# Depthwise convolution taps on TensorE: from 128-wide diagonals built on the chip to four 64x64 tiles with diagonals loaded from DRAM

## The chip, the cores and the metric

One Trainium2 chip, one core of it. The metric is the device time of one execution in microseconds; lower is better. TensorE multiplies, VectorE (DVE), ScalarE (ACT) and GpSimd (POOL) work element by element, SyncE (SP) issues DMAs. The engines run their instruction queues in order and meet by semaphores.

## What is computed

Two stacks of two layers each, on 256 tokens of width 1024, in float32. The first stack has attention, an RWKV recurrence and gated spatial mixing; the second has a feed-forward, a mixer and a second feed-forward in each layer. The change is in the mixer of the second stack, of which this is the part that matters:

```python
q, k, v, c, g = jnp.split(u @ w_in[i], splits, axis=-1)
q = rms_norm_2(q.reshape(B, S, N_HEADS, HEAD_DIM), q_norm[i])
k = rms_norm_2(k.reshape(B, S, KV_HEADS, HEAD_DIM), k_norm[i])
y_attn = window_attention(q, k, v, sink[i], rel_bias) @ w_attn_out[i]
c_val, c_gate = jnp.split(c, 2, axis=-1)
c = c_val * jax.nn.sigmoid(c_gate)
c = depthwise_conv(c, conv_w[i], conv_b[i])     # 31 taps, 512 channels, along the tokens
c = jax.nn.silu(layer_norm_2(c, conv_ln_g[i], conv_ln_b[i]))
y_conv = c @ w_conv_out[i]
g_attn, g_conv = jnp.split(jax.nn.sigmoid(g), 2, axis=-1)
h = h + (g_attn * y_attn + g_conv * y_conv) @ w_o[i]
```

## The kernel before

Activations lie features first: 128 features on the partitions, 256 tokens along a row. The weights come from DRAM in tiles of 128x128, eight to a block (512 KB). A block goes through four engines: SP loads it (`raw`, seven buffers), ScalarE rounds it (`hi`, five buffers), VectorE takes the remainder (`lo`, in place of `raw`), and TensorE does three matmuls for each tile (`lo` by the high part of the activations, `hi` by the high part, `hi` by the low part). ScalarE casts block b + 5 when TensorE has ended block b, since a buffer is free only then; VectorE splits block b + 4 at that point of its queue.

`main_order` lists the work in one order for all engines; each engine's program walks through it. Beside the main line there are side chains (`Flow.chain`): lists of steps with `"next"` between them. At the end of every block `tick` runs each chain on to its next `"next"`, on every engine at its own place in its queue. Attention (`att2_steps`) and the convolution (`conv2_steps`) of the mixer are such chains: what one engine does in step n is used by another in step n or n + 1, and nothing but the queues' order and semaphores ties them.

The convolution's input `Cb` holds four chunks of 128 channels, 286 tokens wide with the padding. Of the 31 taps VectorE does 20 (`CV`), as multiply and add of a shifted row into `cacc`. TensorE does the other 11, each as one float32 matmul of a 128x128 diagonal by 256 columns of `Cb`, accumulated in bank 4 (`CONV`). ScalarE builds the 88 diagonals (identity by a weight), three in each step, in eight buffers. After each pair of chunks VectorE adds the bank to `cacc` (`conv sum`). Then come mean, square, variance, norm, SiLU and the split in high and low part (`ych`, `ycl`), one step each; `conv out` multiplies these by its weights and waits for `("split", l, k // 2)`.

In a mixer the main line is: `c` 0 to 3 (projection of the convolution's input, chain `conv2` started behind `c` 2), `rcol`, `qkv` 0 to 2, `v2`, `qk norm` (matmuls for the norm of queries and keys, then ScalarE and VectorE), attention's chain started, eight `gate2` of two blocks each, `attn out` (four blocks), `conv out` (four blocks), `wo`. Attention's steps, twice: scores, maximum (VectorE), exponential (ScalarE), reciprocal (VectorE), scaling (ScalarE), transposes (`turn`, TensorE), product with the values. Banks of PSUM are taken in turn from pools: `MAIN` is 0, 1, 3 and `ATT2` is 5, 6, 7, 2.

The levels of the RWKV recurrence in the first stack already use tiles of 64x64, in the order and with the banks of this loop (`left` and `right` pick 64 rows of two operands):

```python
for n in range(4):
    for g, s in ((0, 0), (0, 1), (1, 0), (1, 1)):
        rows, into = (slice(64 * t, 64 * t + 64) for t in (s, s ^ g))
        h = 2 * n + g
        i = pe.mm(outs[g][into, n * w:(n + 1) * w], left(h, rows), right(h, rows), True, True)
```

L198 is the helper that issues every matmul, L202 transposes, L250 ScalarE's operations, L205 and L213 VectorE's `tensor_tensor` and `scalar_tensor_tensor`. Most tensors besides the weights lie in one big tile, `arena`, and the profile calls them all by that name.

Of the kernel before, what the change touches and what calls it, by code (L numbers as in the profile page):

```python
# [9 lines left out]
ACT = mybir.ActivationFunctionType  # L10
# [10 lines left out]
L = 2  # L21
# [4 lines left out]
CW, CV = 31, 20  # L26
NT1 = 58 * 8 + 24 * 4 + 64 + 44 * 8 + 22 * 8
# [20 lines left out]
PARG = [("norm_final", 8)]  # L48

# [366 lines left out]
def build(nc, T):  # L416
# [3 lines left out]
    with ctx:  # L420
# [27 lines left out]
        def un(a, n):  # L448
            return ar[:, a * 256:(a + n) * 256]
# [43 lines left out]
        def signal(name, step=1):  # L493
# [10 lines left out]
        d_x = [signal(f"dma_x{i}", 16) for i in range(2)]  # L504
        d_hank = [signal(f"dma_hank{i}", 16) for i in range(8)]
        d_af = [signal(f"dma_first_ada{i}", 16) for i in range(FIRST)]
        d_ada = [signal(f"dma_ada{i}", 16) for i in range(RAWA)]
        d_crow, d_par0, d_par, d_cst0, d_cst1, d_cst, d_lora, d_small, d_b2, d_scr, d_p, d_pp, d_pq, d_out = (
            signal(f"dma_{n}", 16) for n in ("c_row", "par0", "par", "cst0", "cst1", "cst", "lora", "small", "bias2", "scr", "p", "p_out",
                                             "p_back", "out"))  # L510
# [94 lines left out]
        diag = [un(61, 4)[:, i * 128:(i + 1) * 128] for i in range(8)]  # L605
# [14 lines left out]
        def tensor_program(e):  # L620
# [419 lines left out]
            def conv2(l):  # L1040
                taps = [0]

                def step(what, *q):
                    if what == "pe tap":
                        pr, m, j = q
                        if (m, j) == (pr, CV):
                            take(CONV, ("conv", l, pr))
                        d = diag[taps[0] % 8]
                        taps[0] += 1
                        pe.wait_ge(a_cv, ("diag", l, m, j))  # L1050
                        pe.wait_ge(v_main, ("c", l, m))
                        pe.mm(t256(ps(("conv", l, pr)), m - pr), d, Cb[:, m, j:j + 256], j == CV, j == CW - 1).then_inc(
                            pe_cv, ("tap", l, m, j))
                    elif what == "mean":
# [44 lines left out]
            for item in ORDER:  # L1099
# [192 lines left out]
        def vector_program(e):  # L1292
# [365 lines left out]
            def conv2(l):  # L1658
                def w(m, j):
                    return P("conv_w_2", l, j * 4 + m)  # L1660

                def step(what, *q):
                    if what == "taps":
                        pr, j0 = q
                        for j in range(j0, min(j0 + 2, CV)):
                            for m in (pr, pr + 1):
                                o = t256(cacc, m)
                                if j == 0:
                                    v.wait_ge(v_main, ("c", l, m))
                                    x = v.ts(o, Cb[:, m, 0:256], w(m, 0), P("conv_b_2", l, m), MUL, ADD)  # L1670
                                else:
                                    v.wait_ge(v_cv, ("tap", l, m, j - 1))
                                    x = v.stt(o, Cb[:, m, j:j + 256], w(m, j), o, MUL, ADD)
                                x.then_inc(v_cv, ("tap", l, m, j))
                    elif what == "conv sum":
                        pr = q[0]
                        o = cacc[:, pr * 256:(pr + 2) * 256]
                        v.wait_ge(pe_cv, ("tap", l, pr + 1, CW - 1))
                        v.wait_ge(v_cv, ("tap", l, pr + 1, CV - 1))
                        v.tt(o, o, ps(("conv", l, pr)), ADD).then_inc(v_cv, ("conv sum", l, pr), frees=("conv", l, pr))  # L1680
                        if pr == 2:
                            v.wait_ge(v_cv, ("conv sum", l, 2))
                            v.tt(cy2[:, 0:512], cacc[:, 0:512], cacc[:, 512:1024], ADD).then_inc(v_cv, ("conv half", l))
                            v.wait_ge(v_cv, ("conv half", l))
                            v.tt(cy2[:, 0:256], cy2[:, 0:256], cy2[:, 256:512], ADD).then_inc(v_cv, ("conv total", l))
# [51 lines left out]
            for item in ORDER:  # L1737
# [251 lines left out]
                elif what == "gate2":  # L1989
# [3 lines left out]
                    v.wait_ge(pe_main, item)  # L1993
                    v.tt(two(dst), two(ps(item)), bc(var_t, 1, [128, 2, 256]), MUL).then_inc(v_main, item, frees=item)
# [41 lines left out]
        def scalar_program(e):  # L2036
# [262 lines left out]
            def conv2(l):  # L2299
                built = [0]  # L2300

                def step(what, *q):
                    if what == "diag":
                        pr, m, j = q
                        n = built[0]
                        built[0] += 1
                        if n >= 8:
                            a.wait_ge(pe_cv, ("tap", l, *conv_taps[n - 8]))
                        a.wait_ge(d_cst1, "cst1")
                        a.act(diag[n % 8], C("ident"), ACT.Identity, scale=P("conv_w_2", l, j * 4 + m)).then_inc(  # L2310
                            a_cv, ("diag", l, m, j))
                    elif what == "square":
# [20 lines left out]

            conv_taps = [(m, j) for pr in (0, 2) for m in (pr, pr + 1) for j in range(CV, CW)]
# [31 lines left out]
            for item in ORDER:  # L2366
# [201 lines left out]
                elif what == "conv2":  # L2568
                    f.chain(item, conv2_steps(q[0]), conv2(q[0]))
                elif what == "rcol":  # L2570
                    a.wait_ge(pe_main, item)
                    a.act(rcol, adab[:, 0:2], ACT.Copy).then_inc(a_main, item, frees=item)
                elif what == "qkv":
                    l, p = q
                    f.tiles(16 if p < 2 else 8)
                    if p == 2:
# [20 lines left out]
                elif what == "attention2":  # L2597
                    f.chain(("att2", q[0]), att2_steps(q[0]), attention2(q[0]), True)
# [120 lines left out]
        def sync_program(e):  # L2719
# [51 lines left out]
            for item in ORDER:  # L2771
# [82 lines left out]
                elif what == "f first":  # L2854
                    pass
                elif what == "ple":
# [73 lines left out]

def modulation(inputs):
# [12 lines left out]
def program(nc):  # L2944
    def din(name, shape):
# [6 lines left out]
             vmask=din("vmask", (8, 512)), flip=din("flip", (128, 128)), p=din("p", (L, 128, 512)))  # L2952
# [31 lines left out]
```

## Time and profile before

| | |
|---|---|
| median of 3 runs | 2149.69 us (2148.77 to 2149.78) |
| profiled execution | 2149.16 us, span 2147.4 us |
| TensorE busy | 2120.1 us (99%) |
| VectorE busy | 1680.6 us (78%) |
| ScalarE busy | 1265.4 us (59%) |
| GpSimd busy | 13.1 us (1%) |
| granted TensorE clock | 1.00 |
| DMA | 415.12 MB, mean 193 GB/s |

Busy shares are means over stages of different kinds. The span runs from the first to the last instruction; the execution's own time is 1.8 us longer. A float32 matmul has two records in the trace. Rows of the timeline that belong together are merged, with their count; matmuls overlap, so that a merged row ends some 0.28 us after its last start.

### The profile page before, as it was taken

How to read it: one execution, taken by the hardware profiler on the slowest of the kernel's cores; microseconds unless marked ns; L12 is line 12 of the kernel's file. 1: busy time of each engine (PE TensorE's matmuls, PEld its weight loads, DVE VectorE, ACT ScalarE, POOL GpSimd, SP SyncE). 2: the span in 40 equal slices, each digit the busy share in tenths (PEclk: the TensorE clock that was granted, in tenths of full speed). 3: DMA queues.
4: the chain of work that ended last, by engine and by line, in shares of the span. 5: the costliest groups of instructions: out<-in, count | busy, mean ns of one | idle time of the engine just before them, and what ended most of it. 6: DMA issues, size and time to landing. Idle time of an engine off the chain costs nothing.

```text
span 2147.4 us, 38873 instructions
## 1 busy us (share of the span) xinstructions
PE 2120.1 (99%) x16094; PEld 1934.2 (90%) x16094; DVE 1680.6 (78%) x2642; ACT 1265.4 (59%) x2122; POOL 13.1 (1%) x20
## 2 busy tenths in 40 slices
PE   8999999999999999999999999999999999999999
PEld 7898989999998899998888999888898889998888
DVE  7888698887877698776886677887688767878875
ACT  4765556555855755555655567665466545766554
POOL 0000000000000000000000000000000000000000
PEclk9999999999999999999999999999999999999999
DMA  9555577777644477555555533555555553346554
GB/s 371 192 194 174 173 244 258 240 244 276 215 158 168 158 253 231 186 186 186 180 193 187 168 117 132 203 191 191 187 177 191 192 186 128 124 164 205 191 191 129
DMA packets 116371, 415.12 MB, mean 193 GB/s; under 512 B 13105, under 2 KB 16561, under 8 KB 115682
## 3 DMA queue, kind: packets, MB, share of 16 engines
q1 hardware_dynamic: 116194, 412.63, 57.0%
q8 instruction: 127, 2.08, 0.4%
q14 instruction: 50, 0.41, 0.1%
HBM read 409.42 MB, written 3.16 MB: 192 GB/s over the span
## 4 chain that ended last, share of the span: by engine, by line
PE 91%; ACT 4%; DVE 3%; DMA 1%; issue 1%; SPq 0%; ACTq 0%; DVEq 0%
PE bank L198 90%; ACT arena L250 2%; DMA raw<-W 1%; DVE arena L205 1%; DVE lo L205 1%; ACT hi L250 1%; PE bank L202 1%; DVE ada L222 0%; ACT L250 0%; DVE arena L213 0%; ACT L242 0%; DMA xT<-x 0%; DVE h L205 0%; DVE ysl L205 0%; SPq L195 0%
## 5 line engine op out<-in xcount | busy, mean ns | idle before, releaser
L198 PE MATMUL bank<-h,hi 128*128 128x256 f32 (+1 forms) x5344 | 1223.0, 314 | 0.0
L250 ACT ACTIVATE hi<-raw 128x1024 fp32r<-128x1024 f32 x656 | 689.2, 1056 | 563.0 <-PE bank L198 500.7
L198 PE MATMUL bank<-h,lo 128*128 128x256 f32 x3440 | 986.1, 287 | 3.5 <-DVE h L205 3.5
L198 PEld LDWEIGHTS bank<-h,hi 128*128 128x128 f32 x5344 | 880.1, 190 | 67.1 <-issue 2.6
L205 DVE TENSOR_TENSOR lo<-raw,hi 128x1024 fp32r<-128x1024 f32 x656 | 793.1, 1220 | 90.7 <-ACT hi L250 89.8
L198 PEld LDWEIGHTS bank<-h,lo 128*128 128x128 f32 x3440 | 654.6, 190 | 15.1 <-issue 7.0
L198 PE MATMUL bank<-act,hi 128*128 128x512 f32 x1056 | 370.0, 393 | 0.0
L198 PE MATMUL bank<-act,lo 128*128 128x256 f32 x1056 | 294.7, 279 | 0.0
L198 PEld LDWEIGHTS bank<-act,hi 128*128 128x128 f32 x1056 | 197.9, 187 | 47.1
L198 PEld LDWEIGHTS bank<-act,lo 128*128 128x128 f32 x1056 | 197.9, 187 | 0.0
L250 ACT ACTIVATE arena<-arena 128x256 f32<-128x256 f32 (+4 forms) x202 | 98.5, 493 | 158.6 <-DVE arena L205 151.2
L250 ACT ACTIVATE arena<-bank 128x256 f32<-128x256 f32 (+3 forms) x428 | 173.6, 449 | 11.7 <-PE bank L198 10.1
L198 PE MATMUL bank<-arena 64*64 64x64 f32 (+7 forms) x2674 | 165.7, 272 | 7.0 <-ACT arena L250 3.9
L198 PEld LDWEIGHTS bank<-arena 64*64 64x64 f32 (+3 forms) x2674 | 123.6, 145 | 30.1 <-issue 8.5
L205 DVE TENSOR_TENSOR arena<-arena 128x256 f32<-128x256 f32 (+2 forms) x222 | 117.8, 535 | 20.7 <-ACT arena L250 16.9
L213 DVE SCALAR_TENSOR_TENSOR arena<-arena,par 128x256 f32<-128x256 f32 x260 | 116.0, 486 | 19.4 <-ACT arena L250 16.2
L205 DVE TENSOR_TENSOR act<-arena,act 128x256 fp32r<-128x256 f32 x132 | 56.0, 424 | 84.3 <-ACT act L250 83.9
L222 DVE CUSTOM_DVE_ANT_0 ada<-ada,crow,par 128x1024 f32<-128x1024 f32 x80 | 103.5, 1293 | 0.6 <-DMA ada<-WA 0.4
L205 DVE TENSOR_TENSOR arena<-bank,arena 128x256 f32<-128x256 f32 (+2 forms) x181 | 68.7, 423 | 3.6 <-ACT arena L250 3.6
L213 DVE SCALAR_TENSOR_TENSOR xT<-bank,xT 128x256 f32<-128x256 f32 x96 | 40.6, 422 | 35.1 <-PE bank L198 33.5
L250 ACT ACTIVATE act<-arena 128x256 fp32r<-128x256 f32 x132 | 52.9, 401 | 4.8 <-DVE arena L205 4.8
L198 PE MATMUL bank<-ysh,lo 128*128 128x256 f32 x192 | 55.6, 289 | 0.0
(150 smaller groups left out, 1891.6 us busy)
## 6 DMA issues: line engine op xcount, KB each, us to landing
raw<-W SPq DMA_DIRECT2D x664, 512.0 KB, 3.3
ada<-WA SPq DMA_DIRECT2D x80, 512.0 KB, 3.6
arena<-WA SPq DMA_DIRECT2D x16, 512.0 KB, 14.1
p_projected<-arena SPq DMA_DIRECT2D x2, 1024.0 KB, 7.3
arena<-scr SPq DMA_DIRECT2D x16, 128.0 KB, 4.7
arena<-p_projected SPq DMA_DIRECT2D x2, 1024.0 KB, 4.8
xT<-x SPq DMA_DIRECT2D x2, 512.0 KB, 4.9
arena<-lora SPq DMA_DIRECT2D x2, 512.0 KB, 10.3
```

Of the source, the lines that this page charges most:

```text
L198: return self.done(lambda e: e.matmul(out, l, r, start=start, stop=stop, skip_group_check=True))
L202: return self.done(lambda e: e.transpose(out, in_, ident[0:n, 0:n]))
L205: return self.done(lambda e: e.tensor_tensor(out, a, b, op))
L213: return self.done(lambda e: e.scalar_tensor_tensor(out=out, in0=a, scalar=s, in1=b, op0=o0, op1=o1))
L222: return self.done(lambda e: e.tensor_tensor_reduce(out, a, b, 1.0, start, MUL, ADD, total))
L250: return self.done(lambda e: e.activation(out, in_, f, scale=scale, **kw))
```

## The change

Each tap's diagonal is cut in two halves of 64 channels. A tap is now two matmuls of 64x64 by 256 columns. For every second tap the two tiles are those on the array's diagonal, (rows 0-63, outputs 0-63) and (64-127, 64-127), and read `Cb`. For the others they are the two off it, (0-63, 64-127) and (64-127, 0-63), and read a copy of `Cb` in which channels 0-63 and 64-127 of each chunk are exchanged. The two kinds add up in two banks. The copies are made by eight DMAs in all, on ScalarE's queue, when a pair of chunks is there. The diagonals are an input now (`taps`, 1.4 MB a layer) and are loaded by SP at `mixer2`. The 44 matmuls of a pair of chunks stand in one piece: behind `rcol`, and behind `qkv` 0. VectorE adds two banks for each pair, in two steps. `qkv` goes 2, 0, 1 instead of 0, 1, 2, and on ScalarE attention's steps stand ahead of the convolution's.

```diff
 def conv2_steps(l):
-    s = []
-    for pair in (0, 2):
-        todo = [(m, j) for m in (pair, pair + 1) for j in range(CV, CW)]
-        built = []
-        for j in range(0, CV, 2):
-            s += [("taps", pair, j)]
-            if j >= 4:
-                s += [("pe tap", pair, *t) for t in built.pop(0)]
-            built.append(todo[:3])
-            del todo[:3]
-            s += [("diag", pair, *t) for t in built[-1]] + ["next"]
-        assert not any(built), built
-        s += [("conv sum", pair)]
-    return s + ["next", ("mean",), "next", ("square",), "next", ("var",), "next", ("norm",), ("silu",), "next", ("split",)]
+    s = [("taps", 0, 0, 4), "next", ("taps", 0, 4, 8), "next", ("conv sum", 0, 0), "next", ("taps", 0, 8, 12), "next"]
+    s += [("taps", 2, 0, 4), "next", ("conv sum", 2, 0), "next"]
+    for pair, n in ((0, 12), (2, 4)):
+        while n < 2 * CV:
+            s += [("taps", pair, n, min(n + 4, 2 * CV)), "next"]
+            n += 4
+    return s + [("conv total",), "next", ("mean",), "next", ("square",), "next", ("var",), "next", ("norm",), ("silu",), "next", ("split",)]
...
-        s += [("mixer2", l), ("c", l, 0), ("c", l, 1), ("c", l, 2), ("conv2", l), ("c", l, 3), ("c last", l), ("rcol", l)]
-        s += [("qkv", l, p) for p in range(3)] + [("v2", l), ("qk norm", l), ("attention2", l)]
+        s += [("mixer2", l), ("c", l, 0), ("c", l, 1), ("c", l, 2), ("turned", l, 0), ("conv2", l), ("c", l, 3), ("c last", l)]
+        s += [("turned", l, 2), ("rcol", l), ("taps", l, 0), ("qkv", l, 2), ("qkv", l, 0), ("taps", l, 2), ("qkv", l, 1)]
+        s += [("v2", l), ("qk norm", l), ("attention2", l)]
...
+                elif what == "taps":
+                    l, pr = q
+                    outs = [take(ATT2, ("conv", l, pr, d)) for d in range(CG)]
+                    pe.wait_ge(d_taps, ("taps", l))
+                    pe.wait_ge(d_turn[pr // 2], ("turned", l, pr))
+                    pe.wait_ge(v_main, ("c", l, pr + 1))
+                    for m in (pr, pr + 1):
+                        for n in range(CT):
+                            d = tap_turn(m, n)
+                            for r in range(CG):
+                                c = (r + d) % CG
+                                rows, into = slice(CS * r, CS * r + CS), slice(CS * c, CS * c + CS)
+                                i = pe.mm(t256(outs[d], m - pr)[into, :], tapw[rows, m, n, :], Ct[d][rows, m, CV + n:CV + n + 256],
+                                          (m - pr) * CT + n < CG, False)
+                    i.then_inc(pe_main, ("conv", l, pr))
...
+                        pr, first = q
                         o = cacc[:, pr * 256:(pr + 2) * 256]
...
+                        v.wait_ge(pe_main, ("conv", l, pr))
+                        for d in range(first, first + 2):
+                            use = ("conv", l, pr, d)
+                            v.wait_ge(v_cv, before[pr])
+                            v.tt(o, o, ps(use), ADD).then_inc(v_cv, use, frees=use)
+                            before[pr] = last_use[pr] = use
...
+                elif what == "turned":
+                    l, pr = q
+                    a.wait_ge(v_main, ("c", l, pr + 1))
+                    for d in range(1, CG):
+                        n = CS * d
+                        for out, src in ((slice(0, 128 - n), slice(n, 128)), (slice(128 - n, 128), slice(0, n))):
+                            a.dma(Ct[d][out, pr:pr + 2, :], Cb[src, pr:pr + 2, :]).then_inc(d_turn[pr // 2], item)
...
-                    f.chain(("att2", q[0]), att2_steps(q[0]), attention2(q[0]), True)
+                    f.chain(("att2", q[0]), att2_steps(q[0]), attention2(q[0]))
...
+                elif what == "mixer2":
+                    l = q[0]
+                    s.wait_ge(pe_main, ("f down 1", l, 7))
+                    s.dma(tapw.rearrange("p m n i -> p (m n i)"), T["taps"][l]).then_inc(d_taps, ("taps", l))
```

TensorE, layer 0, behind `rcol` (the 128x1 matmuls); before, a block of `qkv` 0 runs to the first three taps, in bank 4:

```order
L198 MATMUL bank2<-cst_72,rs_t_76 128x1 x2
L198 MATMUL bank1<-h_71,lo2_63 128x256
L198 MATMUL bank1<-h_71,hi1_57 128x256 x2
...
L198 MATMUL bank4<-arena_80 128x256 x3
L198 MATMUL bank1<-h_71,lo3_64 128x256
L198 MATMUL bank1<-h_71,hi2_58 128x256 x2
```

and now (22 rows of two matmuls each, banks 5 and 6 in turn, then the weights of `qkv` 2):

```order
L204 MATMUL bank2<-cst_72,rs_t_76 128x1 x2
L204 MATMUL bank5<-arena_80 64x256 x2
L204 MATMUL bank6<-arena_80 64x256 x2
...
L204 MATMUL bank1<-h_71,lo2_63 128x256
L204 MATMUL bank1<-h_71,hi1_57 128x256 x2
```

All 44 matmuls of a pair of chunks now stand ahead of a block of weights, and no taps are left between the later blocks.

ScalarE, layer 0, at attention's first exponential (`arena_80,sml_75<-`, eight times) and the scaling behind it; before, with three diagonals (`<-cst_72,par_73`) in each step:

```order
L250 ACTIVATE hi1_57<-raw3_52 128x1024
L250 ACTIVATE arena_80<-cst_72,par_73 128x128 x3
L250 ACTIVATE sml_75<-sml_75 128x8
L250 ACTIVATE arena_80,sml_75<-arena_80,sml_75 128x256 x8
L250 ACTIVATE hi2_58<-raw4_53 128x1024
L250 ACTIVATE arena_80<-cst_72,par_73 128x128 x3
L250 ACTIVATE arena_80<-arena_80,sml_75 128x256 x8
```

and now:

```order
L256 ACTIVATE hi1_57<-raw3_52 128x1024
L256 ACTIVATE sml_75<-sml_75 128x8
L256 ACTIVATE arena_80,sml_75<-arena_80,sml_75 128x256 x8
L256 ACTIVATE hi2_58<-raw4_53 128x1024
L256 ACTIVATE arena_80<-arena_80,sml_75 128x256 x8
```

The diagonals are gone, and the order of the rest is the same.

VectorE, layer 0, at the end of the convolution's chain; the rows with `bank` are the evictions of `attn out` 0 to 3, one a block, `arena_80<-arena_80 128x1024` is the convolution's norm. Before:

```order
L205 TENSOR_TENSOR arena_80<-arena_80 128x1024
L213 SCALAR_TENSOR_TENSOR arena_80<-arena_80,bank3 128x512
L205 TENSOR_TENSOR lo1_62<-raw1_50,hi3_59 128x1024
L205 TENSOR_TENSOR ycl_86<-arena_80,ych_85 128x512 x2
L213 SCALAR_TENSOR_TENSOR arena_80<-arena_80,bank0 128x512
L205 TENSOR_TENSOR lo2_63<-raw2_51,hi4_60 128x1024
```

and now:

```order
L211 TENSOR_TENSOR lo2_63<-raw2_51,hi4_60 128x1024
L211 TENSOR_TENSOR arena_80<-arena_80 128x1024
L219 SCALAR_TENSOR_TENSOR arena_80<-arena_80,bank1 128x512
L211 TENSOR_TENSOR lo3_64<-raw3_52,hi0_56 128x1024
L211 TENSOR_TENSOR ycl_86<-arena_80,ych_85 128x512 x2
L219 SCALAR_TENSOR_TENSOR arena_80<-arena_80,bank3 128x512
```

Norm and split stand two blocks later; the split is now ahead of the eviction of the last `attn out`.

## Rows read from the trace of the kernel before

**Rows 1.** The page's part 1: busy us, share of the span, instructions.
```profile
PE 2120.1 (99%) x16094; PEld 1934.2 (90%) x16094; DVE 1680.6 (78%) x2642; ACT 1265.4 (59%) x2122; POOL 13.1 (1%) x20
```

**Rows 2.** Busy time by stretches of layer 0's mixer; the first row names the columns.
```profile
core 0: us, PE busy (x) PEld busy (x) DVE busy (x) ACT busy (x) POOL busy (x), PEclk, DMA share, GB/s
1221.48:1249.61 28.13, 28.13 (x210) 27.15 (x210) 21.19 (x40) 15.83 (x31) 0.00 (x0) 1.00 0.35 115
1249.61:1262.18 12.57, 12.57 (x88) 11.21 (x86) 8.27 (x14) 5.90 (x9) 0.00 (x0) 1.00 0.36 123
1262.18:1282.44 20.26, 20.26 (x156) 19.32 (x155) 19.55 (x37) 17.01 (x44) 0.00 (x0) 1.00 0.41 131
1282.44:1311.22 28.78, 28.78 (x221) 26.53 (x219) 24.51 (x44) 20.77 (x51) 0.00 (x0) 1.00 0.33 110
1311.22:1334.40 23.18, 22.18 (x182) 20.95 (x181) 15.10 (x19) 19.78 (x27) 0.00 (x0) 1.00 0.41 136
```

**Rows 3.** Timeline: three taps between blocks (PE), and casts at blocks' ends (ACT).
```profile
1229.15 1.46 PE L198 MATMUL bank<-arena 128*128 128x256 f32 x6
1233.32 1.46 PE L198 MATMUL bank<-arena 128*128 128x256 f32 x6
...
1337.54 1.06 ACT L250 ACTIVATE hi<-raw 128x1024 fp32r<-128x1024 f32 x1 [1.82 <-PE bank L198]
1340.42 1.06 ACT L250 ACTIVATE hi<-raw 128x1024 fp32r<-128x1024 f32 x1 [1.82 <-PE bank L198]
```

**Rows 4.** Timeline of TensorE around one RWKV level, and its matmuls by form.
```profile
132.31 0.40 PE L198 MATMUL bank<-h,hi 128*128 128x256 f32 x2
132.64 1.57 PE L198 MATMUL bank<-arena 64*64 64x64 f32 x64
...
134.36 0.40 PE L198 MATMUL bank<-h,hi 128*128 128x256 f32 x2
...
L198 PE MATMUL bank<-arena 64*64 64x128 f32 x32 | 1.1, 269 | 0.0
L198 PE MATMUL bank<-arena 64*64 64x64 f32 x32 | 0.7, 224 | 0.0
```

**Rows 5.** Timeline: VectorE's and ScalarE's part of attention, first half.
```profile
1253.91 1.68 DVE L213 SCALAR_TENSOR_TENSOR arena<-arena,par 128x1024 f32<-128x1024 f32 x2 [8.10 <-ACT arena L250]
1256.64 1.67 DVE L213 SCALAR_TENSOR_TENSOR arena<-arena,par 128x256 f32<-128x256 f32 x4
1258.23 1.22 DVE L205 TENSOR_TENSOR lo<-raw,hi 128x1024 fp32r<-128x1024 f32 x1
1263.34 2.48 DVE L213 SCALAR_TENSOR_TENSOR arena<-bank,arena 128x512 f32<-128x512 f32 x4 [0.58 <-PE bank L198]
1268.91 2.28 DVE L225 TENSOR_REDUCE sml<-arena 128x8 f32<-128x2048 f32 x1
1277.95 0.21 DVE L219 RECIPROCAL sml<-sml 128x8 f32<-128x8 f32 x1
...
1278.81 3.29 ACT L250 ACTIVATE arena<-arena,sml 128x256 f32<-128x256 f32 x8
```

**Rows 6.** Timeline of ScalarE: the second half's scaling.
```profile
1307.09 3.29 ACT L250 ACTIVATE arena<-arena,sml 128x256 f32<-128x256 f32 x8
```

**Rows 7.** Timeline: cast ahead of SiLU (ACT), and both splits behind it (DVE).
```profile
1326.39 1.04 ACT L250 ACTIVATE hi<-raw 128x1024 fp32r<-128x1024 f32 x1
...
1330.53 0.69 DVE L205 TENSOR_TENSOR ycl<-arena,ych 128x512 fp32r<-128x512 f32 x1 [1.84 <-ACT ych L250]
1332.18 0.69 DVE L205 TENSOR_TENSOR ycl<-arena,ych 128x512 fp32r<-128x512 f32 x1 [0.96 <-ACT ych L250]
```

**Rows 8.** Timeline of TensorE: the convolution's variance, layer 0.
```profile
1322.38 0.67 PE L198 MATMUL bank<-arena,cst 128*128 128x256 f32 x2 [0.99 <-DVE arena L205]
```

**Rows 9.** DMA issues (KB each, median us to landing); gating of the second chunk.
```profile
raw<-W SPq DMA_DIRECT2D x664, 512.0 KB, 3.3
arena<-scr SPq DMA_DIRECT2D x16, 128.0 KB, 4.7
arena<-lora SPq DMA_DIRECT2D x2, 512.0 KB, 10.3
...
1217.29 0.43 DVE L213 SCALAR_TENSOR_TENSOR arena<-arena 128x256 f32<-128x256 f32 x1 [0.76 <-ACT arena L250]
```

More of the change, by code:

```diff
@@ L26 @@
 CW, CV = 31, 20
+CG = 2
+CT, CS = CW - CV, 128 // CG
 NT1 = 58 * 8 + 24 * 4 + 64 + 44 * 8 + 22 * 8
@@ L48, with tap_turn @@
 PARG = [("norm_final", 8)]
+def tap_turn(m, n):
+    return (m % 2 * CT + n) % CG
 def par_columns():
@@ L504, in build @@
         d_x = [signal(f"dma_x{i}", 16) for i in range(2)]
+        d_turn = [signal(f"dma_turned{i}", 16) for i in range(2)]
         d_hank = [signal(f"dma_hank{i}", 16) for i in range(8)]
@@ L507, in build @@
         d_ada = [signal(f"dma_ada{i}", 16) for i in range(RAWA)]
-        d_crow, d_par0, d_par, d_cst0, d_cst1, d_cst, d_lora, d_small, d_b2, d_scr, d_p, d_pp, d_pq, d_out = (
+        d_crow, d_par0, d_par, d_cst0, d_cst1, d_cst, d_lora, d_small, d_b2, d_scr, d_p, d_pp, d_pq, d_taps, d_out = (
             signal(f"dma_{n}", 16) for n in ("c_row", "par0", "par", "cst0", "cst1", "cst", "lora", "small", "bias2", "scr", "p", "p_out",
-                                             "p_back", "out"))
+                                             "p_back", "taps", "out"))
         negw0, halfa0 = sml[:, 32:40], sml[:, 40:48]
@@ L604, in build @@
         cacc, cyc, cy2 = un(16, 4), un(20, 4), un(24, 4)
-        diag = [un(61, 4)[:, i * 128:(i + 1) * 128] for i in range(8)]
+        Ct = [Cb] + [ar[:, 73 * 256 + i * 1144:73 * 256 + (i + 1) * 1144].rearrange("p (m t) -> p m t", m=4) for i in range(CG - 1)]
+        tapw = un(78, 11)[:, 0:4 * CT * CS].rearrange("p (m n i) -> p m n i", m=4, n=CT)
         pf, pfh, pfl = un(49, 2), alias("pfh", 51, 2), alias("pfl", 57, 2)
@@ L1040, in conv2 @@
             def conv2(l):
-                taps = [0]
                 def step(what, *q):
[L1044 to L1054, printed above, removed]
+                    if what == "mean":
                         o = take(CONV, ("cmean", l))
@@ L1658, in conv2 @@
             def conv2(l):
+                before, last_use = {}, {}
                 def w(m, j):
@@ L1663, in step @@
                     if what == "taps":
[L1664 to L1674, printed above, removed]
+                        pr, first, last = q
@@ new lines, in step @@
+                        for n in range(first, last):
+                            j, m = n // 2, pr + n % 2
+                            o = t256(cacc, m)
+                            if j == 0:
+                                v.wait_ge(v_main, ("c", l, m))
+                                x = v.ts(o, Cb[:, m, 0:256], w(m, 0), P("conv_b_2", l, m), MUL, ADD)
+                            else:
+                                v.wait_ge(v_cv, last_use.pop(pr) if pr in last_use else ("tap", l, m, j - 1))
+                                x = v.stt(o, Cb[:, m, j:j + 256], w(m, j), o, MUL, ADD)
+                            x.then_inc(v_cv, ("tap", l, m, j))
+                            before[pr] = ("tap", l, m, j)
@@ L1675, in step @@
                     elif what == "conv sum":
-                        pr = q[0]
+                        pr, first = q
                         o = cacc[:, pr * 256:(pr + 2) * 256]
[L1678 to L1685, printed above, removed]
+                        v.wait_ge(pe_main, ("conv", l, pr))
@@ new lines, in step @@
+                        for d in range(first, first + 2):
[3 more added lines that the diff above has]
+                            before[pr] = last_use[pr] = use
+                    elif what == "conv total":
+                        v.wait_ge(v_cv, ("tap", l, 3, CV - 1))
+                        v.tt(cy2[:, 0:512], cacc[:, 0:512], cacc[:, 512:1024], ADD).then_inc(v_cv, ("conv half", l))
+                        v.wait_ge(v_cv, ("conv half", l))
+                        v.tt(cy2[:, 0:256], cy2[:, 0:256], cy2[:, 256:512], ADD).then_inc(v_cv, ("conv total", l))
@@ L1993, in vector_program @@
                     v.wait_ge(pe_main, item)
+                    v.wait_ge(pe_main, ("conv", l, 2))
                     v.tt(two(dst), two(ps(item)), bc(var_t, 1, [128, 2, 256]), MUL).then_inc(v_main, item, frees=item)
@@ L2299, in conv2 @@
             def conv2(l):
-                built = [0]
                 def step(what, *q):
[L2303 to L2312, printed above, removed]
+                    if what == "square":
                         a.wait_ge(v_cv, ("cmean", l))
@@ L2332, in conv2 @@
                 return step
-            conv_taps = [(m, j) for pr in (0, 2) for m in (pr, pr + 1) for j in range(CV, CW)]
             def merge(name, l, m, h):
@@ L2928, in stream, with tap_weights @@
     return out.reshape(nblk, 128, BT * 128)
+def tap_weights(inputs):
+    w = np.asarray(inputs["conv_w_2"], np.float32).reshape(L, CW, 4, CG, CS)
+    out = np.zeros((L, CG, CS, 4, CT, CS), np.float32)
+    i = np.arange(CS)
+    for m in range(4):
+        for n in range(CT):
+            for r in range(CG):
+                out[:, r, i, m, n, i] = w[:, CV + n, m, (r + tap_turn(m, n)) % CG, :]
+    return out.reshape(L, 128, 4 * CT * CS)
 def modulation(inputs):
@@ L2951, in program @@
              oneh=din("oneh", (32, 512)), relb=din("relb", (32, 8)),
-             vmask=din("vmask", (8, 512)), flip=din("flip", (128, 128)), p=din("p", (L, 128, 512)))
+             vmask=din("vmask", (8, 512)), flip=din("flip", (128, 128)), p=din("p", (L, 128, 512)), taps=din("taps", (L, 128, 4 * CT * CS)))
     T["out"] = nc.dram_tensor("out", [128, 2048], F32, kind="ExternalOutput").ap()
@@ L2978 @@
         crow=np.ascontiguousarray(crow), lnb=np.ascontiguousarray(np.repeat(ln[:, None, :], 128, axis=1)), bs=bs,
-        oneh=oneh, relb=np.ascontiguousarray(inputs["rel_bias_2"]), vmask=vmask, flip=flip,
+        taps=tap_weights(inputs), oneh=oneh, relb=np.ascontiguousarray(inputs["rel_bias_2"]), vmask=vmask, flip=flip,
         p=np.stack([features_first(inputs["p_2"][l, 0]) for l in range(L)]))
```

2 lines of the change are left out of this document (1 added, 1 removed).

## The prediction

> **What bounds the kernel now.** I read the page first: TensorE is busy for 2120.1 of 2147.4 us, VectorE for 78% [rows 1]. The reader is to see that a microsecond taken from TensorE's queue is a microsecond of the end, as long as the others keep up. So the table by stretches comes next, for the mixer of layer 0 of the second block, where the convolution's taps run [rows 2]. TensorE is never idle there but for 1.0 us in the last stretch. VectorE, though, is busy for 19.55 of the 20.26 us between the first scores and the first transposes of attention: it follows TensorE with almost nothing to spare. Layer 1 repeats layer 0 565.5 us later, so everything is counted twice.
>
> I call eight weight tiles a block, as the kernel does. Without taps a block takes TensorE 2.88 us (the `hi` casts of ScalarE, each waiting for the end of a block, start 2.88 us apart); with three taps between two blocks the period is 4.17 us [rows 3]. So a tap costs (4.17 - 2.88) / 3 = 0.43 us, 0.435 with the switches.
>
> **What is removed from TensorE.** 11 taps x 4 chunks x 2 layers = 88 matmuls x 0.435 = 38.3 us, 18 of each layer's 44 before the q/k norm, 26 behind it.
>
> **What is added.** 176 matmuls of 64x64 by 256 columns, in four blocks of 44. The trace has this very pattern: the levels of the RWKV inverse (`quarters`) issue 64x64 tiles in the same order, two into one bank and two, with halves exchanged, into another, in float32 too. One such burst has 16 matmuls of 64 columns and 16 of 128 (32 records each) [rows 4]. At 0.427 us for 256 columns (a tap without its share of the switches) a column is 1.67 ns; one after another, 16 x 64 + 16 x 128 columns would be 5.1 us. The burst costs 134.36 - 132.31 less three steps of 0.12 us, which the weight matmuls between take anyway, 1.7 us. With four at once it is 1.28 us plus 0.4 us of switch and tail; with two at once 2.56 us already. So four run at once, and a new block is 44 x 0.427 / 4 + 0.4 = 5.1 us, four of them 20.4 us. TensorE alone thus gains 38.3 - 20.4 = 17.9 us.
>
> On a rule that speaks against this: of the burst the rows show 1.7 us, with both row halves writing one bank. The Trainium skill (TensorEngine Tiling (Array Packing), Restrictions and Gotchas) says that different row tiles can't access one PSUM bank at the same time. By that rule two would run at once, a block would be 9.8 us, and the sum 18.8 us higher; this trace does not agree with it.
>
> Also gone: 88 diagonals on ScalarE. Added on VectorE: four sums of bank and accumulator instead of two in each layer, near 0.6 us each. Neither is on TensorE's path by itself. The load of the diagonals (1.4 MB on SP's queue) stands behind a wait that ends with the same matmul as the block before it, so SP loses nothing; it is used 20 us later, and the weights, at 3.3 us to landing [rows 9], are asked for seven blocks ahead. I cost both at nothing.
>
> **Where cover is lost.** The steps of attention and convolution run once a block on every engine. Taps stretched a block to 4.17 us for TensorE; now it is 2.88. VectorE does in such a block a `lo` split (1.13 us), four taps (1.59) and half an eviction (0.3), 3.0 us, and more where attention has its steps. I count from T, the start of the q/k norm's matmuls (1249.61 before).
>
> First transposes: VectorE's chain starts at T + 4.3, when ScalarE has the norm [rows 5]. From there VectorE has no gap: norm 1.6, two blocks of split and taps and an eviction 6.0, a split 1.13, so it is at the scores at T + 13.1, while TensorE, without the 1.8 us of taps, starts them at T + 10.8. Evictions of scores 2.4, taps 1.6, split 1.1, maximum 2.8: T + 21.0 (22.2 before). From there to the reciprocal are taps, eviction, split, taps, split: 6.4 us, as in the rows; ScalarE's eight scalings add 3.3. The probabilities are ready at T + 30.9. TensorE is there, five blocks after scores, at T + 27.2. Before, the scalings ended at 1282.10 and the transposes began at 1282.44 [rows 2, 5]: 0.3 us to spare. New wait: 3.7 us.
>
> Second transposes: counted on in the same way, scores at T + 35.5, maximum T + 44.9, ScalarE's exponentials from T + 46.3 (behind the `hi` cast that waits for TensorE) to 50.4, reciprocal 51.9, scalings 55.3; TensorE is there at T + 53.8. Before, 0.8 us were to spare (1310.39 against 1311.22) [rows 2, 6]. New wait: 1.5 us.
>
> End of the convolution: the new steps put SiLU at step 27 and the split at step 28, where they were 25 and 26, and step 28 is the last block of `attn out`. ScalarE comes to SiLU only when TensorE has ended block 27, and then does cast, table load, SiLU, copy. From the start of that cast to the end of the first `ycl` are 4.8 us, to the second 6.5 (1326.39 to 1332.87) [rows 7]. TensorE has 2.88 us of block 28 left and 0.72 us of `conv out` before it wants the second half: 6.5 - 3.6 = 2.9 us of wait, where there was none.
>
> The variance of the convolution waited 1.0 us before [rows 8]; `ysh` and a table load no longer stand in its way, and I count 0.4 us.
>
> **Sum.** Each layer: taps -19.15, blocks +10.2, waits 3.7 + 1.5 + 2.9 + 0.4 - 1.0 = +7.5: -1.4 us. Two layers: -2.8 us. The profiled execution took 2149.16 us with a span of 2147.4; against the median of the runs, 2149.69, I forecast 2147.0 us. TensorE's saving is thus mostly handed to waits. For each of the new waits the bounds are nothing and twice its size: 0 to 16 us a layer; I take the worked values, since 0.3 and 0.8 us of slack before are measured.
>
> **The first copy with halves exchanged** can start at 1217.7, when VectorE has the second chunk gated; TensorE wants it behind `rcol`, at 1222.1 [rows 2, 9]. There are 4.4 us. Nearest rows: 3.3 us for the weights, 4.7 for 128 KB from DRAM, 10.3 for `lora`. By the first two it costs 0 to 0.3 us a layer, by the last 5.9. It is 143 KB, near the second; I take nothing.
>
> **The rivals.**
> - A, the waits as worked out: 2147.0, itself between 2142 and 2152. 0.60.
> - B, VectorE and ScalarE keep up better, so that one or more waits stay away: with none, 2149.7 - 17.9 = 2131.8; with only that of `conv out`, 2137.6. For it: 0.7 us of VectorE's stretch was idle. Against: the slack before was 0.3 us where TensorE now comes 3.9 us (nine taps) sooner. 0.20.
> - C, slower: the copies land late. At 10.3 us, 2147.0 + 11.8 = 2158.8; it decides once they need over 8 us. For it: 128 pieces of 1.1 KB beside the weights' stream; against: 128 KB in 4.7. 0.15.
> - D, the tiles do not overlap as in the RWKV burst, two at once: 2147.0 + 18.8 = 2165.8. The change would then save TensorE nothing at all. Against: [rows 4]. 0.05.
>
> **Numbers.** 0.2% is 4.3 us, about what a measurement of this kernel can tell from no change. Below 2145.4: 0.18 of A, 0.17 of B, 0.35. Above 2154.0: 0.02 of A, 0.12 of C, all of D, 0.19. Between, 0.46. The range of 8 in 10 takes in A and the edges of B and C: 2138 to 2156.
>
> **What would show it.** Four bursts of 5.1 us with 44 matmuls each; TensorE idle 3 to 4 us ahead of the first transposes behind scalings of ScalarE, 1 to 2 us ahead of the second, about 3 us in two pieces at `conv out` behind VectorE's `ycl`; VectorE without a gap from T + 4.3 to the maximum. TensorE's busy time down by about 18 us and its idle time up by 15. I am wrong if the first transposes wait for nothing, if a burst takes over 7 us, if TensorE waits for the copy, or if after a wait of 3.7 us the granted clock, 1.00 in all stretches here [rows 2], is found at 1.2 GHz for a while, which no row of before prices.

## The result and the profile after

| | before | after |
|---|---|---|
| median | 2148.81 us (20 runs, 2148.16 to 2149.78) | 2152.58 us (20 runs, 2150.70 to 2156.82) |
| profiled execution, span | 2147.4 us | 2149.9 us |
| granted TensorE clock | 1.00 | 0.997 |

The ratio is 1.0019, with an interval of 1.0012 to 1.0025: 3.8 us slower, where 2.7 us faster was forecast (2147.0 against the 2149.69 known then). The page of the changed kernel has these rows (part 1; the first line of the chain that ended last; two of the DMA issues):

```profile
PE 2110.8 (98%) x16270; PEld 1921.0 (89%) x16270; DVE 1683.1 (78%) x2646; ACT 1238.0 (58%) x2032; POOL 13.1 (1%) x20
...
PE 87%; ACT 6%; DVE 5%; DMA 1%; issue 1%; SPq 0%; ACTq 0%; DVEq 0%
...
arena<-taps SPq DMA_DIRECT2D x2, 1408.0 KB, 8.3
...
arena<-arena ACTq DMA_DIRECT2D x8, 143.0 KB, 2.6
```

TensorE's busy time fell from 2120.1 us [rows 1] by 9.3 us only, where about 18 were to go. Busy time counts slow matmuls as well as many, so this is the first sign that something other than waiting took time back. The copies land in 2.6 us.

TensorE's timeline in layer 0, its waits and the landmarks that answer to [rows 2, 4, 7, 8]. The number in brackets is the idle time ahead of the row and what ended it:

```profile
1221.26 4.98 PE L204 MATMUL bank<-arena 64*64 64x256 f32 x88
...
1251.08 2.36 PE L204 MATMUL bank<-arena,cst 128*128 128x512 f32 x6
...
1282.37 3.26 PE L208 MATMUL bank<-cst,arena 128*128 128x128 f32 x16 [3.80 <-ACT arena L256]
...
1308.33 1.94 PE L208 MATMUL bank<-cst,arena 128*128 128x128 f32 x16 [0.95 <-ACT arena L256]
...
1324.82 0.67 PE L204 MATMUL bank<-arena,cst 128*128 128x256 f32 x2 [0.56 <-DVE arena L211]
...
1333.45 0.36 PE L204 MATMUL bank<-ych,lo 128*128 128x256 f32 x1 [2.22 <-DVE ycl L211]
1335.01 0.58 PE L204 MATMUL bank<-ych,lo 128*128 128x256 f32 x1 [0.39 <-DVE ycl L211]
```

The burst has no wait ahead of it and takes 4.98 us. T, the start of the q/k norm, is 1251.08, and this execution was 0.75 us ahead of the other up to `rcol`, so T came 2.2 us later by the change. All the new waits are there, 3.8, 0.95, 0.56 and 2.2 + 0.4 us. One thing in these rows is not a wait: the same sixteen transposes take 3.26 us behind the long wait and 1.94 behind the short one.

Windows of 1 us of the same kernel say why; the column to read is PEclk, the granted clock, the third number from a row's end (0.50 is 1.2 GHz, 1.00 is 2.4 GHz):

```profile
core 0: us, PE busy (x) PEld busy (x) DVE busy (x) ACT busy (x) POOL busy (x), PEclk, DMA share, GB/s
1281.00:1282.00 1.00, 0.00 (x0) 0.00 (x0) 1.00 (x2) 1.00 (x4) 0.00 (x0) 1.00 0.24 94
1282.00:1283.00 1.00, 0.63 (x5) 0.66 (x6) 1.00 (x4) 1.00 (x3) 0.00 (x0) 0.90 0.00 0
1283.00:1284.00 1.00, 1.00 (x7) 1.00 (x6) 1.00 (x3) 1.00 (x2) 0.00 (x0) 0.50 0.06 16
...
1285.00:1286.00 1.00, 1.00 (x6) 1.00 (x6) 1.00 (x3) 1.00 (x4) 0.00 (x0) 0.50 0.00 0
1286.00:1287.00 1.00, 1.00 (x10) 1.00 (x9) 1.00 (x3) 1.00 (x3) 0.00 (x0) 0.90 0.00 0
1287.00:1288.00 1.00, 1.00 (x11) 1.00 (x10) 1.00 (x2) 0.09 (x1) 0.00 (x0) 1.00 0.00 0
...
1334.00:1335.00 1.00, 0.62 (x4) 0.33 (x2) 0.73 (x2) 1.00 (x2) 0.00 (x0) 0.50 0.01 4
...
1336.00:1337.00 1.00, 1.00 (x7) 1.00 (x6) 0.69 (x1) 0.00 (x0) 0.00 (x0) 0.50 0.07 16
```

The clock is at half for 3.4 us from 1282.8 on, behind the wait of 3.80 us, and again for 3.4 us in the second stretch, behind 2.22 us; it stays at 1.00 behind 0.95 us. At half the clock a window holds 6 or 7 records of matmuls instead of 10 or 11, so such a stretch costs about half of what TensorE works in it, 1.7 us in the first and, with 0.39 us of the second wait inside it, 1.5 in the other. Layer 1 has the same two stretches. The Trainium skill (TensorE: Matmul & The Clock Gate, Why this matters for your kernels) tells to avoid long idle gaps between bursts of matmuls, since the clock goes back to half behind them. The trace agrees for 3.80 us, and here the clock also fell behind 2.22 us.

What held the first transposes is seen in the chain that ended last, followed through this place (start, us, what; VectorE from the scores' eviction, whose row also holds four taps, to the reciprocal, then the scalings on ScalarE):

```profile
1264.63 3.98 DVE arena L219 x8
1268.60 1.14 DVE lo L211
1269.74 2.21 DVE sml L231
...
1272.54 1.58 DVE arena L219 x4
1274.12 0.60 DVE arena L211
1274.73 1.13 DVE lo L211
1275.86 1.58 DVE arena L219 x4
1277.44 1.14 DVE lo L211
...
1278.69 0.21 DVE sml L225
...
1279.34 2.90 ACT arena L256 x7
```

VectorE has no gap there. Between maximum and reciprocal stand eight taps (two rows of 1.58 us), an eviction of `gate2` (0.60) and two splits of weights. The taps are the convolution's work, in front of attention's.

### The profile page after: what moved, and what is told of

Its sections match the earlier page's. It is cut to its first block, busy times and chain, and to the rows that moved or that the text cites. A ratio compares the mean times of both kernels' runs of the same rounds, so it can differ in the third digit from the quotient of the medians.

```text
span 2149.9 us, 39148 instructions
## 1 busy us (share of the span) xinstructions
PE 2110.8 (98%) x16270; PEld 1921.0 (89%) x16270; DVE 1683.1 (78%) x2646; ACT 1238.0 (58%) x2032; POOL 13.1 (1%) x20
## 4 chain that ended last, share of the span: by engine, by line
PE 87%; ACT 6%; DVE 5%; DMA 1%; issue 1%; SPq 0%; ACTq 0%; DVEq 0%
PE bank L204 86%; ACT arena L256 4%; DVE lo L211 1%; DVE arena L219 1%; ACT hi L256 1%; DVE arena L211 1%; PE bank L208 1%; DMA raw<-W 1%; ACT L256 0%; DVE ada L228 0%; DMA xT<-x 0%; DVE sml L231 0%; ACT L248 0%; ACT ych L256 0%; DVE h L211 0%
## 5 line engine op out<-in xcount | busy, mean ns | idle before, releaser
L204 PE MATMUL bank<-arena 64*64 64x64 f32 (+7 forms) x2850 | 142.1, 278 | 6.9 <-ACT arena L256 3.9
L204 PEld LDWEIGHTS bank<-arena 64*64 64x64 f32 (+2 forms) x2850 | 105.5, 141 | 31.0 <-issue 8.8
L219 DVE SCALAR_TENSOR_TENSOR arena<-arena,par 128x256 f32<-128x256 f32 x260 | 115.9, 485 | 14.0 <-ACT arena L256 10.8
## 6 DMA issues: line engine op xcount, KB each, us to landing
arena<-WA SPq DMA_DIRECT2D x16, 512.0 KB, 13.8
```

The costliest lines, as they stand in the source:

```text
L204: return self.done(lambda e: e.matmul(out, l, r, start=start, stop=stop, skip_group_check=True))
L219: return self.done(lambda e: e.scalar_tensor_tensor(out=out, in0=a, scalar=s, in1=b, op0=o0, op1=o1))
```

## The experiments

The theory: the change took from TensorE what it should; the time went into two waits in each layer, and each of them costs more than its length, since the clock is at half behind it. Rivals: that the 64x64 bursts are themselves dearer than they look or slow what runs beside them; that the tiles do not run four at once; that the waits come of the bursts or the added sums and not of where the steps stand.

| run | median us | ratio to before (interval) |
|---|---|---|
| e1_warm | 2147.76 | 0.9997 (0.9988 to 1.0005) |
| e2_ahead | 2144.54 | 0.9983 (0.9974 to 0.9992) |
| e3_merged | 2142.99 | 0.9975 (0.9966 to 0.9985) |
| e4_both | 2135.00 | 0.9938 (0.9926 to 0.9950) |
| e5_straight | 2172.11 | 1.0106 (1.0092 to 1.0120) |
| e6_late | 2157.70 | 1.0039 (1.0025 to 1.0053) |
| e7_22 | 2131.38 | 0.9918 (0.9905 to 0.9932) |

### e1_warm: TensorE busy in the waits

The changed kernel with added matmuls on constants, whose result nobody reads, in front of the two long waits.

```diff
+            def warm(use, n):
+                o = take(CONV, use)
+                pe.wait_ge(d_cst, "cst")
+                for i in range(n):
+                    pe.mm(o[:, 0:256], C("ones"), C("cos"), True, True)
...
                     elif what == "turn":
+                        if p == 0:
+                            warm(("warm", l, 0), 8)
...
                     l, p = q
+                    if p == 0:
+                        warm(("warm", l, 1), 6)
```

Expected:

> The changed kernel, plus matmuls whose result nobody reads, into the idle bank 4: eight float32 ones of 256 columns (3.5 us) ahead of the first transposes of attention and six (2.6 us) ahead of conv out. They fill TensorE's two long waits and shorten neither. Theory (the missing 3.1 us of each layer are the granted clock, down to half for some 3.4 us behind each of the two long waits): the clock stays at 1.00, the transposes take 1.9 us instead of 3.3, and the time falls by 6 us, to 2146.5. Rival (they are other work or waits that stretched): the time stays at 2152.6.

Measured: 2147.76 us, 4.8 us less than the changed kernel, with 28 matmuls more. Its timeline on TensorE:

```profile
1280.03 3.62 PE L204 MATMUL bank<-cst 128*128 128x256 f32 x16
...
1283.99 1.94 PE L208 MATMUL bank<-cst,arena 128*128 128x128 f32 x16 [0.35 <-ACT arena L256]
...
1331.08 2.75 PE L204 MATMUL bank<-cst 128*128 128x256 f32 x12
1335.02 0.38 PE L204 MATMUL bank<-ych,lo 128*128 128x256 f32 x1 [0.47 <-DVE ycl L211]
```

The transposes still come when ScalarE lets them, but they take 1.94 us again, and the clock is 1.00 throughout both mixers. Nothing was made shorter here but the time behind the waits, so the clock's cost is shown: 4.8 us by the medians. In the profiled executions the way from T to the first matmul of `wo` is 93.22 us in both layers, where the changed kernel took 95.87 and 95.54: 5.0 us in all.

### e2_ahead: taps taken out of attention's way

The changed kernel with another plan of VectorE's steps: none of the taps between maximum and reciprocal, 16 in one step ahead of them (step 8); as many steps as before.

```diff
+    for step in range(1, 22 + 1):
...
+        elif step not in (3, 6, 10, 11, 13):
+            for _ in range({8: 4}.get(step, 1)):
+                if todo:
+                    p, n = todo.pop(0)
+                    s += [("taps", p, n, n + 4)]
```

Expected:

> The changed kernel with twelve of VectorE's taps of each layer moved: step 8 of the convolution's chain does sixteen instead of four, in VectorE's wait for the q/k norm, and steps 10, 11 and 13, between that wait and attention's first reciprocal, do none. Nothing else moves. Theory (VectorE's queue is what makes the first transposes wait): that wait of 3.8 us and the clock behind it (1.6 us) go, the second wait of 1 us stays, conv out still waits; 2 x 5.4 = 10.8 us less, 2141.8. Rival (ScalarE's chain or the semaphores set it): less than 3 us.

Measured: 2144.54 us, 8.0 less than the changed kernel. TensorE's waits, and the same wait in layer 1 (1891.53):

```profile
1280.36 1.94 PE L208 MATMUL bank<-cst,arena 128*128 128x128 f32 x16 [0.87 <-ACT arena L256]
...
1329.83 0.36 PE L204 MATMUL bank<-ych,lo 128*128 128x256 f32 x1 [2.22 <-DVE ycl L211]
1331.38 0.38 PE L204 MATMUL bank<-ych,lo 128*128 128x256 f32 x1 [0.60 <-DVE ycl L211]
...
1891.53 0.36 PE L204 MATMUL bank<-ych,lo 128*128 128x256 f32 x1 [2.22 <-DVE ycl L211]
```

And its windows, behind that wait in layer 0 and in layer 1:

```profile
1332.00:1333.00 1.00, 1.00 (x11) 1.00 (x10) 1.00 (x1) 0.00 (x0) 0.00 (x0) 1.00 0.06 16
...
1894.00:1895.00 1.00, 1.00 (x7) 1.00 (x7) 0.76 (x1) 0.00 (x0) 0.00 (x0) 0.50 0.00 0
```

The first wait is 0.87 us instead of 3.80, and no half clock follows. The wait at `conv out` is the same to 0.01 us in both layers, and the clock falls in one and not in the other. The gain was forecast as 10.8 us and came out as 8.0, and the profiled execution is 1.5 us under the median: whether the clock falls behind the 2.2 us differs by place and, it seems, by run.

### e3_merged: two steps fewer

The changed kernel with each first sum in the step of taps beside it, so that the split stands at step 26 instead of 28. Taps are still in attention's way.

```diff
-    s = [("taps", 0, 0, 4), "next", ("taps", 0, 4, 8), "next", ("conv sum", 0, 0), "next", ("taps", 0, 8, 12), "next"]
-    s += [("taps", 2, 0, 4), "next", ("conv sum", 2, 0), "next"]
-    for pair, n in ((0, 12), (2, 4)):
+    s = [("taps", 0, 0, 4), "next", ("taps", 0, 4, 8), "next", ("conv sum", 0, 0), ("taps", 0, 8, 12), "next"]
+    s += [("taps", 2, 0, 4), "next", ("taps", 0, 12, 16), "next", ("conv sum", 2, 0)]
+    for pair, n in ((0, 16), (2, 4)):
```

Expected:

> The changed kernel with the two steps that only add banks merged with steps that do taps, so that the split comes at step 26 as in the kernel before, not at 28. Theory: the wait at conv out (2.6 us) and the clock behind it (1.6 us) go, the first transposes wait as before; 2 x 4.2 = 8.4 us less, 2144.2. Rival (conv out would wait for ScalarE's SiLU anyway, whatever the step): no change.

Measured: 2142.99 us, 9.6 less than the changed kernel. There is no wait at `conv out` and none at the variance; the first transposes wait 3.80 us as before. The clock behind that wait, though, was at half for longer than in the changed kernel's execution:

```profile
1281.00:1282.00 1.00, 0.00 (x0) 0.00 (x0) 1.00 (x3) 1.00 (x4) 0.00 (x0) 1.00 0.87 344
1282.00:1283.00 1.00, 0.00 (x0) 0.00 (x0) 1.00 (x2) 1.00 (x4) 0.00 (x0) 0.52 0.25 98
1283.00:1284.00 1.00, 0.56 (x3) 0.59 (x4) 1.00 (x4) 1.00 (x3) 0.00 (x0) 0.50 0.00 0
...
1287.00:1288.00 1.00, 1.00 (x7) 1.00 (x7) 1.00 (x3) 1.00 (x3) 0.00 (x0) 0.50 0.00 0
1288.00:1289.00 1.00, 1.00 (x7) 1.00 (x7) 1.00 (x2) 0.24 (x1) 0.00 (x0) 0.56 0.00 0
```

Here it fell while TensorE was still idle, and stayed down until 1288.9: 5.4 us of work at half the clock. From the first to the second transposes this takes 2.6 us more than at full clock, behind the same wait that cost 1.6 in the other execution. Layer 1 is alike, with 2.4 us. This profiled execution is at 2145.52 us, 2.5 above the median.

### e4_both

Both edits together: quiet steps 10, 11 and 13, sums merged, 20 steps of taps.

Expected:

> Both edits of the schedule together: taps ahead of attention, and the sums merged with tap steps. Theory: only the second transposes wait, about 1 us a layer, the clock never falls; what is left is TensorE's saving of 17.9 us less 2 us: 2132. Rival (some other wait takes their place, since VectorE has no less to do): 2140 or more.

Measured: 2135.00 us, 17.6 less than the changed kernel and 13.8 less than before. The waits of TensorE that are left in layer 0:

```profile
1222.34 4.98 PE L204 MATMUL bank<-arena 64*64 64x256 f32 x88 [2.05 <-DVE arena L219]
...
1280.53 1.94 PE L208 MATMUL bank<-cst,arena 128*128 128x128 f32 x16 [0.87 <-ACT arena L256]
```

The clock is 1.00 in every stretch of both mixers. The two gains, 8.0 and 9.6, add up to the 17.6 measured, so the two waits don't depend on each other. The sum of the expectation, worked out again, is 2148.8 - 17.9 + 2 = 2132.9 and not 2132, so 2.1 us are missing in the median. The profiled execution has 2.05 us of them in the wait ahead of the first burst, which only its layer 0 shows. The row names VectorE, but the transfers tell it apart: the two copies were issued at 1215.95, the one landed 2.7 us after its issue and the other 5.6 us, at 1222.1, just ahead of the burst; in layer 1 the same two took 2.3 and 2.6 us. So a copy landed late there. Whether one does in the other executions of this kernel is not shown.

### e5_straight: only two tiles at once

Both tiles of every tap on the array's diagonal; the banks alternate as before.

```diff
-                                c = (r + d) % CG
+                                c = r
...
-                                i = pe.mm(t256(outs[d], m - pr)[into, :], tapw[rows, m, n, :], Ct[d][rows, m, CV + n:CV + n + 256],
+                                i = pe.mm(t256(outs[d], m - pr)[into, :], tapw[rows, m, n, :], Ct[0][rows, m, CV + n:CV + n + 256],
...
-                out[:, r, i, m, n, i] = w[:, CV + n, m, (r + tap_turn(m, n)) % CG, :]
+                out[:, r, i, m, n, i] = w[:, CV + n, m, r, :]
```

Expected:

> The changed kernel with both tiles of every tap on the array's diagonal (rows and outputs of the same 64 channels, read from the convolution's input itself; the two banks still alternate). It computes the same. Theory (the burst runs four 64x64 tiles at once, 44 matmuls in 5.0 us): now only the two tiles of one tap can run at once, 22 pairs by 0.435 us as a 128x128 tap took before, 9.6 to 9.9 us a burst, so 4 x 4.7 = 18.8 us more: 2171 us against 2152.6 of the changed kernel. Rival: two tiles at once is all that happens and the 5.0 us come of something else in the burst: 2152 us, the bursts as before. Second rival: tiles of one bank run one after the other: 18 to 20 us a burst, some 2210 us.

Measured: 2172.11 us, 19.5 more than the changed kernel. One burst on its timeline:

```profile
1222.60 9.72 PE L204 MATMUL bank<-arena 64*64 64x256 f32 x88
```

9.72 against 4.98 us, four times 4.74 is 19.0 us. So in the changed kernel four tiles do run at once, and the two tiles off the diagonal, which need the exchanged copy, are what allows it. The Trainium skill (TensorEngine Tiling (Array Packing), Restrictions and Gotchas) has it that different row tiles can't access one bank of PSUM at the same time. Both tiles of a tap write one bank, from different row halves to different halves of the partitions. The pace of this run alone, 0.44 us a tap, would also fit two tiles of different banks side by side. That of the changed kernel does not: 44 matmuls in 4.98 us are four at once in two banks, so two row halves write each bank together. This case does not agree with that page of the Trainium skill as it is put.

### e6_late: the loss without the change

The kernel before, with nothing but two empty steps ahead of the mean.

```diff
-    return s + ["next", ("mean",), "next", ("square",), "next", ("var",), "next", ("norm",), ("silu",), "next", ("split",)]
+    return s + ["next", "next", "next", ("mean",), "next", ("square",), "next", ("var",), "next", ("norm",), ("silu",), "next", ("split",)]
```

Expected:

> The kernel before with two empty steps ahead of the convolution's mean, so that norm and split stand two blocks later as in the changed kernel, and nothing else changed: no 64x64 tile, no copy, no reordering. Theory (the loss comes of the places of the steps and of the clock behind the wait, not of the tiles): a wait of about 2.6 us at the convolution's output in each layer, half the clock for some 3 us behind it (1.6 us), so 2 x 4.2 = 8.4 us more, 2157 us against 2148.8. If only the wait counts and the clock is nothing: 2154 us. Rival (the waits of the changed kernel come of its bursts and of VectorE's added sums): 2149 us.

Measured: 2157.70 us, 8.8 more than before. Its timeline at `conv out`:

```profile
1335.57 0.46 PE L198 MATMUL bank<-ych,lo 128*128 128x256 f32 x1 [2.22 <-DVE ycl L205]
```

Two windows of 1 us behind it:

```profile
1336.00:1337.00 1.00, 1.00 (x6) 0.80 (x4) 0.62 (x2) 1.00 (x2) 0.00 (x0) 0.50 0.04 12
...
1338.00:1339.00 1.00, 1.00 (x6) 1.00 (x6) 0.81 (x1) 0.00 (x0) 0.00 (x0) 0.50 0.00 0
```

and two of layer 1, where its wait of 2.23 us ended at 1904.81:

```profile
1906.00:1907.00 1.00, 0.63 (x3) 0.64 (x4) 1.00 (x3) 0.53 (x1) 0.00 (x0) 0.50 0.00 0
...
1911.00:1912.00 1.00, 1.00 (x7) 1.00 (x6) 0.97 (x3) 0.73 (x1) 0.00 (x0) 0.50 0.47 94
```

The wait of 2.22 us and the half clock behind it come without any 64x64 tile, copy or other order: two places in a list of steps make them. They are worth 4.4 us a layer by the medians, where the waits alone would be 1.8 to 2.4 (2.22, in layer 1 another 0.61 behind it, less 0.43 that the variance now waits less). The two layers are not alike: from T to `wo` layer 0 took 3.7 us more than before and layer 1 took 5.5, since there the clock stayed down for 6.8 us instead of 3.4.

### e7_22: nine taps on TensorE

e4_both with `CV` at 22 and the added multiply-adds in steps 2, 5 and 8, where VectorE waited for the bursts. The edit against e4_both:

```diff
-CW, CV = 31, 20
+CW, CV = 31, 22
...
-            for _ in range({8: 4}.get(step, 1)):
+            for _ in range({2: 2, 5: 2, 8: 4}.get(step, 1)):
```

Expected:

> The version with both edits (steps moved out of attention, sums merged) and nine taps on TensorE instead of eleven, 22 on VectorE, whose added multiply-adds (eight a layer, 3.4 us) fill steps two, five and eight. It computes the same. Theory (VectorE has idle time at its waits for the bursts, 3.5 and 2.1 us in each layer, and TensorE's time is what counts): 36 matmuls a burst instead of 44, 4 x 0.9 = 3.6 us less than 2135.0: 2131.5 us. Rival (VectorE's queue reaches attention's steps later, and TensorE waits for it): 3.4 us a layer brought back less what idle time takes up, 2138 to 2142 us.

Measured: 2131.38 us, the fastest of all, 0.8% under the kernel before. TensorE's timeline in layer 0:

```profile
1223.21 4.12 PE L204 MATMUL bank<-arena 64*64 64x256 f32 x72
...
1279.66 1.94 PE L208 MATMUL bank<-cst,arena 128*128 128x128 f32 x16 [0.87 <-ACT arena L256]
...
1304.00 1.95 PE L208 MATMUL bank<-cst,arena 128*128 128x128 f32 x16 [0.96 <-ACT arena L256]
```

A burst is 0.86 us shorter, 3.4 us for four of them, and the waits are those of e4_both: VectorE's 3.4 us more in each layer are hidden.

## Why the prediction failed

**Where the saving goes: right.** T came 2.2 us later, 2.4 were worked out (44 x 0.427 / 4 + 0.4 twice, less 18 taps). A burst took 4.98 us where 5.1 was predicted; rival D, by which it is twice that, is what e5_straight shows: 9.72 us a burst and 2172.11 us. It was right to read the four at once off [rows 4].

**The copies and the loads: right.** 2.6 us to landing where 4.4 were free; the changed kernel waits for none. Rival C shows once in the profiled executions, in layer 0 of e4_both.

**The waits: right in place, cause and size.** Predicted and measured: first transposes 3.7 and 3.80; second 1.5 and 0.95; `conv out` 2.9 and 2.22 + 0.39; variance 0.4 and 0.56. Together 8.5 and 7.9 us in layer 0; layer 1 has 7.5, without the 0.39. VectorE had no gap from the scores to the reciprocal, as said. e2_ahead shortens the first to 0.87 us and e3_merged takes that of `conv out` away; they give back 8.0 and 9.6 us. Rival B, that they stay away, did not come.

**The step that failed is the sum:** "waits 3.7 + 1.5 + 2.9 + 0.4 - 1.0 = +7.5: -1.4 us" a layer prices a wait at its own length. It lacks the granted clock behind it. The last sentence of the prediction names that as a way to be wrong, but with no row for it the price was taken as nothing, and neither the likeliest case nor a rival held it. In the profiled execution these are four stretches of 3.4 us at half the clock, which made TensorE's work 6.0 us longer. Taking them away brings back 4.8 us by the medians of e1_warm: at full clock TensorE is sooner at the second half of `conv out` and waits there instead.

The account, from the profiled executions: forecast were -1.4 us a layer. From `rcol` to the first matmul of `wo` it was 124.44 us in both layers before (1221.48 to 1345.92), and 126.22 (1220.73 to 1346.95) and 125.89 after: +1.8 and +1.5 us, 3.2 in all, against 3.8 by the medians. T came 0.2 us earlier than worked out, so the rest lies behind T. These are the windows from T to `wo` in layer 0, before, e4_both, e2_ahead and after; TensorE has the same matmuls in the last three, and the clock is 1.00 in the first three:

```profile
1249.61:1345.92 96.31, 95.31 (x735) 89.53 (x734) 78.85 (x128) 68.92 (x137) 0.00 (x0) 1.00 0.40 131
1252.16:1338.45 86.29, 84.46 (x685) 79.87 (x685) 76.54 (x124) 63.08 (x115) 0.00 (x0) 1.00 0.45 147
1252.00:1342.28 90.28, 85.07 (x685) 79.95 (x685) 80.36 (x133) 62.01 (x114) 0.00 (x0) 1.00 0.43 140
1251.08:1346.95 95.87, 87.95 (x685) 82.75 (x684) 80.88 (x134) 62.23 (x114) 0.00 (x0) 0.96 0.39 132
```

- Taps: 96.31, less 26 taps (11.3) and with 1.83 us of waits instead of 0.99, is 85.8; e4_both took 86.29. The 26 taps together were worth some 0.4 us less than 26 times 0.435.
- Waits: e2_ahead waits in three more places than e4_both, 3.38 us in all, and took 3.99 us more. So a wait costs some 0.2 us beyond the idle time that its row shows, and the changed kernel, which has the same three besides those of e4_both, pays 0.6 for them. The idle time itself is 0.6 under the forecast, so these two cancel.
- Clock: 86.29, with the longer first wait (2.93), the three waits (0.56 + 2.22 + 0.39) and their 0.6, is 93.0; measured are 95.87. The clock's part is 2.9 us (3.2 by the count of its windows), and 3.1 in layer 1 by the same sum.

Layer 0 is then -1.4 - 0.2 + 0.4 - 0.6 + 0.6 + 2.9 = +1.7, where +1.8 was measured. Each part is a difference of executions, good to some 0.1 or 0.2 us. The clock is by far the largest. Without it the change would have come out about even: e1_warm is at 0.9997 of before, with 1 inside its interval.

**The bounds.** "Nothing and twice its size" for the waits give a range that holds the result, for a reason that wasn't theirs: each wait is within 0.7 us of the worked value, and the clock used the room.

**What could have been done.** Both waits come from where steps stand, not from the tiles: e6_late makes one in the kernel before, for 8.8 us, and e4_both, with the same tiles and another list of steps, is 13.8 us faster than before. Of the 17.9 us that TensorE was to gain, it keeps 13.8.

## What to carry to other kernels

A wait of the engine that bounds the kernel is to be priced with what its clock does afterwards: here a wait of 2.2 or 3.8 us cost 1.3 to 2.7 us more by the clock in all places but one, and waits under 1 us nothing by the clock. So when a change makes such an engine faster, its gain is kept only if the lists of steps beside it are moved as well; look for an operation with no hurry (here taps of the convolution) that stands between two of a chain that has some. Work of 64x64 can fill the array four at a time if the operand with exchanged halves is there, which a small transfer off the path can supply.

## What the runs showed that was not expected

- The clock fell to 1.2 GHz behind idle times of 3.80 us and of 2.22 us (in some places with another of 0.4 to 0.6 us right behind it), and in no profile behind 0.87 to 0.96 us, nor behind the single 2.05 us of e4_both. Of the profiles of the changed kernel, e2_ahead, e3_merged, e5_straight and e6_late, it fell in 6 of 6 places behind the long wait and in 7 of 8 behind 2.22 us; the eighth is layer 0 of e2_ahead.
- Behind the same wait of 3.80 us it stayed down for 3.4 us in the changed kernel and for 6.8 us in both layers of e3_merged; behind the one of 2.22 us for 3.4 us in most places and for 6.8 in layer 1 of e6_late. It fell either after TensorE had begun again or while it was idle.
- Runs of a kernel with such waits spread more: 2150.70 to 2156.82 us for the changed kernel, where before had 2148.16 to 2149.78.
- Useless matmuls in a wait made the kernel 4.8 us faster.
